# Transposing the gated values of a SwiGLU on VectorE in 32x32 squares instead of on TensorE

## The chip, the cores and the metric

The kernel runs on one core of one Trainium2 chip. The metric is device time in microseconds, the median of several executions; lower is better. One more execution was taken with the hardware profiler. Its rows are what this document reads.

## The reference

Two layers of a decoder trunk over 256 tokens of width 1024, all in float32. Each layer is an attention part (two groups of heads) and then a gated feed-forward part, each between two RMS norms:

```python
D_MODEL = 1024; SEQ = 256; DEPTH = 2
D_FF = -(-8 * D_MODEL // (3 * 256)) * 256          # 2816
...
    x = x + rms_norm(jnp.einsum('bse,ed->bsd', mix, w_out), g_attn_post)
    h = rms_norm(x, g_ffn_pre)
    f = jax.nn.silu(jnp.einsum('bsd,df->bsf', h, w_gate)) * jnp.einsum('bsd,df->bsf', h, w_up)
    x = x + rms_norm(jnp.einsum('bsf,fd->bsd', f, w_down), g_ffn_post)
```

The change lies between the last two lines: f comes out with tokens on partitions, and the product with w_down needs it with its 2816 features on partitions.

## The kernel before, in words

**Products.** Tokens stand in two tiles of 128 (t = 0, 1). Every float32 product is made of three passes of TensorE: an operand is split into a high part and the rest (suffixes h and l), and hh, hl and lh are added up in PSUM (`multiply`, L1083). The weights come in 46 blocks per layer of 1 MB each (128 partitions x 2048 floats), numbered 0 to 45: blocks 13 to 34 are gate and up, 35 to 45 are down. A block is loaded by SP's queue into one of three raw places (L318), ScalarE writes its high part (`hi`, L494) into one of four slots, VectorE subtracts to get the low part (`lo`, L729), and then TensorE may use it, first for tile 0, then for tile 1. `hi` of a block waits until the block four slots back has been used; a load waits until `lo` has read the block three places back. So `after(L, b)` in ScalarE's and VectorE's programs means: the blocks whose slot comes free when TensorE is through with block b. In most of the feed-forward part that is block b + 4. In the down part, where the slots are counted from the end, it is nothing after 34 and 35, block 38 after 36, and blocks 39, 40 and 41 after 37.

**The feed-forward part.** The 2816 features go in six chunks c = 0 to 5: five of 512 features with four blocks each (gate, gate, up, up), and one of 256 features with two. For each chunk and tile ScalarE applies silu to the gate bank (`silus`, L597), VectorE multiplies by up (`swiglu`, L909) and leaves f[t] in SBUF. TensorE then transposes f[t] in 128x128 pieces into PSUM (`f_transposed`, which calls `transpose`, L1123): four pieces per chunk and tile, two in the last chunk. It does this inside the first block of the next chunk, after tile 0 and after tile 1. ScalarE copies the PSUM bank to the high part (`hiT`, L521), VectorE subtracts to get the low part (`loT`, L756). fT (and actT for the last chunk) then is the stationary operand of the down product. The last four down blocks (42 to 45) run for tile 0 first and then for tile 1, and the last two chunks' results are needed only there.

**Order.** Every engine runs its own program, written out by hand, in order; they meet at semaphores. A wait in an engine's program holds up all that stands behind it.

Of the kernel before, what the change touches and what calls it, by code (L numbers as in the profile page):

```python
# [25 lines left out]
P = 128  # L26
D = 1024
T = 2
# [114 lines left out]
for j in range(2):  # L143
    HOLDS[4 + j].append(("ht", 0, j, 1))
    for g in (SWA, MOBA):
        for r in range(3):
# [2 lines left out]
HOLDS[6] += [("ht", 0, 0, 0), ("qk", 0, 0), ("qk", 1, 0), ("qk", 0, 1), ("qk", 1, 1), ("qk", 2, 0), ("qk", 2, 1),  # L149
             ("qk", 3, 0), ("qk", 3, 1), ("mix", SWA, 0), ("mix", SWA, 1), ("mix", MOBA, 0), ("mix", MOBA, 1),  # L150
             ("ht", 1, 0, 0)]
HOLDS[6] += [("ft", c, 0) for c in range(FFN_CHUNKS)]
HOLDS[7] += [("ht", 0, 1, 0), ("pv", SWA, 0), ("pv", SWA, 1), ("pv", MOBA, 0), ("pv", MOBA, 1), ("ht", 1, 1, 0)]
HOLDS[7] += [("ft", c, 1) for c in range(FFN_CHUNKS)]
BANK_OF = {name: b for b in range(8) for name in HOLDS[b]}


def trunk(nc, x_in, b_in, g_attn_pre, g_attn_post, g_moba, g_swa, sinks_in,
# [3 lines left out]
    with ExitStack() as ctx:  # L162
        def sb(name, shape, dt=F32):
            return ctx.enter_context(nc.sbuf_tensor(name, shape, dt))

        def sem(name):
            return ctx.enter_context(nc.semaphore(name))
# [25 lines left out]
        still = work[:, 9, :].bitcast(BF16)  # L193
        silu = [work[:, 6 + t, :] for t in range(T)]
        f = [work[:, 8 + t, :] for t in range(T)]
        v = {MOBA: sb("v_moba", [P, T, GROUP]), SWA: sb("v_swa", [P, T, KV])}
        qT = {g: sb(f"qT_{g}", [P, 4, SEQ]) for g in (MOBA, SWA)}
        kT = {MOBA: sb("kT_0", [P, 4, SEQ]), SWA: sb("kT_1", [P, 1, SEQ])}
# [59 lines left out]
        o_scaled = sem("o_scaled")  # L258
        eps_added = sem("eps_added")
        half_ready = sem("half_ready")  # L260
        pool_step = sem("pool_step")
        dve_step = sem("dve_step")

# [12 lines left out]
        def turned(L, key):  # L276
# [6 lines left out]
        SINK_ARG, SINK_EXP = Order([0, 1]), Order([0, 1])  # L283
        HIT = Order([("ht", 0, 0, 0), ("ht", 0, 0, 1), ("ht", 0, 1, 0), ("ht", 0, 1, 1), ("mix", SWA, 0),
                     ("mix", SWA, 1), ("mix", MOBA, 0), ("mix", MOBA, 1), ("ht", 1, 0, 0), ("ht", 1, 0, 1),
                     ("ht", 1, 1, 0), ("ht", 1, 1, 1)] + [("ft", c, t) for c in range(FFN_CHUNKS) for t in range(T)])

        def transposed(name):

            if name[0] == "ht":  # L290
                return actT, 4 * name[3], 4, name[2]
            if name[0] == "mix":
                return actT, 4 * name[1], 4, name[2]
            if 4 * name[1] < KF_OWN:
                return fT, 4 * name[1], 4, name[2]
            return actT, 4 * name[1] - KF_OWN, KF - 4 * name[1], name[2]

        def tokens(t):
            return slice(t * P, (t + 1) * P)
# [181 lines left out]
        def _(act):  # L481
# [29 lines left out]
            def after(L, b):  # L511

                for c in freed_by(b):
                    hi(L, c)

            def hiT(L, name):

                b = BANK_OF[name]
                dst, k, nk, t = transposed(name)
                act.wait_ge(full[b], HELD[b].done(L, name))  # L520
                nc.scalar.activation(dst["h"][:, k:k + nk, tokens(t)],  # L521
                                     bank[b][:, 0:nk * P].rearrange("p (k n) -> p k n", k=nk), ACT.Copy
                                     ).then_inc(hiT_ready, 1)
                HIT.tick(name)

            def sum_x(L, ph, t):
                into = junk[ph][t] if (L, ph) != (0, 0) else work[:, t, :].bitcast(BF16)
                nc.scalar.activation(into, x[:, t, :], ACT.Square, scale=D ** -0.5,
                                     accum_out=ss_x[:, t:t + 1]).then_inc(squares_x, 1)
                SQ_X.tick((ph, t))  # L530

            def sum_y(L, ph, t, halves=(0, 1)):
                for c in halves:
                    name = ("down" if ph else "out", t, c)
                    b = BANK_OF[name]
                    act.wait_ge(full[b], HELD[b].done(L, name))
                    nc.scalar.activation(y[t][:, c, :], bank[b][:], ACT.Square, scale=D ** -0.5,  # L537
                                         accum_out=ss_y[:, t, c:c + 1]).then_inc(squares_y, 1)
                    SQ_Y.tick((ph, t, c))
# [75 lines left out]
            for L in range(depth):  # L615
# [68 lines left out]
                after(L, 16)  # L684
                for c in range(1, FFN_CHUNKS):
                    b = FIRST_FFN + 4 * c
                    hiT(L, ("ft", c - 1, 0))
                    after(L, b)
                    hiT(L, ("ft", c - 1, 1))
                    silus(L, c, 0)  # L690
                    silus(L, c, 1)
                    for q in range(1, 2 if c == FFN_CHUNKS - 1 else 4):
                        after(L, b + q)
                hiT(L, ("ft", FFN_CHUNKS - 1, 0))
                after(L, FIRST_DOWN)
                hiT(L, ("ft", FFN_CHUNKS - 1, 1))
                for b in range(FIRST_DOWN + 1, NB - 4):
                    after(L, b)
                sum_y(L, 1, 0)
                if L < depth - 1:  # L700
                    hi(L + 1, 0)
# [14 lines left out]
        def _(dve):  # L716
# [15 lines left out]
            def after(L, b):  # L732
                for c in freed_by(b):
                    lo(L, c)
# [16 lines left out]
            def loT(L, name):  # L751

                b = BANK_OF[name]
                dst, k, nk, t = transposed(name)
                dve.wait_ge(hiT_ready, HIT.done(L, name))
                nc.vector.tensor_tensor(dst["l"][:, k:k + nk, tokens(t)],  # L756
                                        bank[b][:, 0:nk * P].rearrange("p (k n) -> p k n", k=nk),
                                        dst["h"][:, k:k + nk, tokens(t)].bitcast(F32), ALU.subtract
                                        ).then_inc(drained[b], 1)
# [140 lines left out]
            def swiglu(L, c, t):  # L900
                n = min(BANK, FF - c * BANK)
                b = BANK_OF["up", c, t]
                dve.wait_ge(full[b], HELD[b].done(L, ("up", c, t)))
                bg = BANK_OF["gate", c, t]
                dve.wait_ge(drained[bg], HELD[bg].done(L, ("gate", c, t)) + 1)
                if c:
                    bt = BANK_OF["ft", c - 1, t]
                    dve.wait_ge(full[bt], HELD[bt].done(L, ("ft", c - 1, t)))
                nc.vector.scalar_tensor_tensor(f[t][:, 0:n], bank[b][:, 0:n], rstd_x[:, t:t + 1], silu[t][:, 0:n],  # L909
                                               ALU.mult, ALU.mult).then_inc(drained[b], 1)  # L910

            nc.vector.memset(still, 0.0).then_inc(still_ready, 1)
            dve.wait_ge(xT_in_done[0], 16)
# [9 lines left out]
            for L in range(depth):  # L923
# [74 lines left out]
                after(L, 14)  # L998
                swiglu(L, 0, 0)
                after(L, 15)  # L1000
                swiglu(L, 0, 1)
                after(L, 16)
                for c in range(1, FFN_CHUNKS):
                    b = FIRST_FFN + 4 * c
                    end = b + (1 if c == FFN_CHUNKS - 1 else 3)
                    loT(L, ("ft", c - 1, 0))
                    after(L, b)
                    loT(L, ("ft", c - 1, 1))
                    for q in range(b + 1, end):
                        after(L, q)  # L1010
                    swiglu(L, c, 0)
                    swiglu(L, c, 1)
                    after(L, end)
                loT(L, ("ft", FFN_CHUNKS - 1, 0))
                after(L, FIRST_DOWN)
                loT(L, ("ft", FFN_CHUNKS - 1, 1))
                for b in range(FIRST_DOWN + 1, NB - 4):
                    after(L, b)
                scale_y(L, 1, 0)
                update_x(L, 1, 0)  # L1020
                if L < depth - 1:
# [18 lines left out]
        def _(pe):  # L1040
# [141 lines left out]
                pe.wait_ge(o_scaled, O_SCALED.done(L, (g, t)))  # L1182
                transpose(L, ("mix", g, t), lambda q: o[t][:, q * P:(q + 1) * P], 4)

            def f_transposed(L, c, t):
                b = BANK_OF["up", c, t]
                pe.wait_ge(drained[b], HELD[b].done(L, ("up", c, t)) + 1)
                transpose(L, ("ft", c, t), lambda q: f[t][:, q * P:(q + 1) * P], min(4, KF - 4 * c))

            def rows_landed(L, ph, t):  # L1190
                for half in range(2):
# [18 lines left out]
            for L in range(depth):  # L1210
# [125 lines left out]
                multiply(L, 1, b + 3)  # L1336
                for c in range(1, FFN_CHUNKS):
                    b = FIRST_FFN + 4 * c
                    multiply(L, 0, b)
                    f_transposed(L, c - 1, 0)  # L1340
                    multiply(L, 1, b)
                    f_transposed(L, c - 1, 1)
                    for q in range(1, 2 if c == FFN_CHUNKS - 1 else 4):
                        multiply(L, 0, b + q)
                        multiply(L, 1, b + q)
                for t in range(T):
                    landed(L, ("ft", FFN_CHUNKS - 2, t))
                for b in range(FIRST_DOWN, NB - 4):
                    multiply(L, 0, b)
                    if b == FIRST_DOWN:  # L1350
                        f_transposed(L, FFN_CHUNKS - 1, 0)
                    multiply(L, 1, b)
                    if b == FIRST_DOWN:
                        f_transposed(L, FFN_CHUNKS - 1, 1)
                for t in range(T):
                    landed(L, ("ft", FFN_CHUNKS - 1, t))
                for b in range(NB - 4, NB):
                    multiply(L, 0, b)
                for b in range(NB - 4, NB):
# [37 lines left out]
```

## Time and profile before

| what | value |
|---|---|
| median of 3 runs | 598.49 us (598.32 to 598.55) |
| the profiled execution: its own time | 598.48 us |
| its span, first to last instruction | 596.7 us |
| TensorE busy | 585.4 us, 98% of the span |
| VectorE busy | 362.0 us, 61% |
| ScalarE busy | 292.8 us, 49% |
| granted TensorE clock | 0.998 of full speed |
| loads | 107.26 MB, mean 180 GB/s |

The profiled execution lies 1.8 us above its span, and 0.01 us from the median, so a microsecond taken from the span is a microsecond taken from the median. Busy shares are averages over stages. Matmuls are pipelined: a recorded duration of one is its passage, not the time that it costs its successor; start to start is what counts there.

### The profile page before, as it was taken

How to read it: one execution, taken by the hardware profiler on the slowest of the kernel's cores; microseconds unless marked ns; L12 is line 12 of the kernel's file. 1: busy time of each engine (PE TensorE's matmuls, PEld its weight loads, DVE VectorE, ACT ScalarE, POOL GpSimd, SP SyncE). 2: the span in 40 equal slices, each digit the busy share in tenths (PEclk: the TensorE clock that was granted, in tenths of full speed). 3: DMA queues.
4: the chain of work that ended last, by engine and by line, in shares of the span. 5: the costliest groups of instructions: out<-in, count | busy, mean ns of one | idle time of the engine just before them, and what ended most of it. 6: DMA issues, size and time to landing. Idle time of an engine off the chain costs nothing.

```text
span 596.7 us, 7657 instructions
## 1 busy us (share of the span) xinstructions
PE 585.4 (98%) x3004; PEld 486.1 (81%) x3004; DVE 362.0 (61%) x469; ACT 292.8 (49%) x417; POOL 42.1 (7%) x68
## 2 busy tenths in 40 slices
PE   7999999999999999999999999999999999999996
PEld 4878887888888889888888888788888888898884
DVE  4888965947536546165497987567645536533632
ACT  6574663755453444153446745665554453424420
POOL 1100001410000000000120100034000000000000
PEclk9999999999999999999999999999999999999999
DMA  8872632437655541559266343507565555342701
GB/s 313 328 239 104 230 142 107 168 125 284 235 168 186 210 154 59 211 224 331 80 239 212 142 159 122 196 6 278 194 244 172 200 171 186 137 184 99 281 1 70
DMA packets 18291, 107.26 MB, mean 180 GB/s; under 512 B 2768, under 2 KB 3024, under 8 KB 6608
## 3 DMA queue, kind: packets, MB, share of 16 engines
q1 hardware_dynamic: 17968, 105.73, 48.9%
q10 hardware_dynamic: 288, 1.05, 0.5%
q8 instruction: 24, 0.39, 0.3%
q14 instruction: 11, 0.09, 0.0%
HBM read 105.72 MB, written 1.05 MB: 179 GB/s over the span
## 4 chain that ended last, share of the span: by engine, by line
PE 85%; DVE 6%; ACT 6%; DMA 1%; issue 1%; DVEq 0%; POOLq 0%; POOL 0%; ACTq 0%
PE bank L1083 75%; PE bank L1123 4%; ACT work L559 3%; DVE w_l L729 3%; PE bank L1173 2%; DVE bank L835 2%; PE bank L1108 2%; ACT w_h L494 2%; PE bank L1148 1%; DMA work<-in_x_first_transposed 1%; DVE actT_l L756 1%; DVE top L835 0%; ACT actT_h L521 0%; ACT work L575 0%; DVE neg_max L839 0%
## 5 line engine op out<-in xcount | busy, mean ns | idle before, releaser
L729 DVE TENSOR_TENSOR w_l<-raw,w_h 128x2048 fp32r<-128x2048 f32 x91 | 207.7, 2290 | 144.2 <-ACT w_h L494 144.1
L494 ACT ACTIVATE w_h<-raw 128x2048 fp32r<-128x2048 f32 x91 | 173.9, 1917 | 143.0 <-PE bank L1083 118.1
L1083 PE MATMUL bank<-w_h,actT_h 128*128 128x512 f32 (+1 forms) x600 | 232.3, 387 | 0.2
L1083 PE MATMUL bank<-w_h,actT_l 128*128 128x512 f32 (+1 forms) x600 | 225.9, 377 | 0.0
L1083 PE MATMUL bank<-w_l,actT_h 128*128 128x512 f32 (+1 forms) x600 | 225.2, 375 | 0.0
L1083 PEld LDWEIGHTS bank<-w_h,actT_h 128*128 128x128 f32 x600 | 113.1, 189 | 22.6 <-issue 2.7
L1083 PEld LDWEIGHTS bank<-w_h,actT_l 128*128 128x128 f32 x600 | 112.9, 188 | 21.2
L1083 PEld LDWEIGHTS bank<-w_l,actT_h 128*128 128x128 f32 x600 | 113.2, 189 | 18.3
L1083 PE MATMUL bank<-w_h,fT_h 128*128 128x512 f32 x160 | 49.8, 392 | 0.0
L1083 PE MATMUL bank<-w_h,fT_l 128*128 128x512 f32 x160 | 49.3, 389 | 0.0
L1083 PE MATMUL bank<-w_l,fT_h 128*128 128x512 f32 x160 | 49.3, 389 | 0.0
L1123 PE MATMUL bank<-ident,work 128*128 128x128 f32 x316 | 46.4, 274 | 2.3 <-ACT work L559 1.5
L1123 PEld LDWEIGHTS bank<-ident,work 128*128 128x128 f32 x316 | 37.4, 141 | 11.5 <-ACT work L559 4.2
L559 ACT ACTIVATE work<-bank,neg_max 128x128 f32<-128x128 f32 (+1 forms) x64 | 26.0, 425 | 33.1 <-DVE neg_max L839 33.1
L1083 PEld LDWEIGHTS bank<-w_l,fT_h 128*128 128x128 f32 x160 | 30.0, 188 | 6.3
L1083 PEld LDWEIGHTS bank<-w_h,fT_l 128*128 128x128 f32 x160 | 30.0, 188 | 6.3
L1083 PEld LDWEIGHTS bank<-w_h,fT_h 128*128 128x128 f32 x160 | 29.5, 188 | 5.8
L444 POOL TENSOR_TENSOR norms<-norms,constants 128x1 f32<-128x1 f32 x8 | 6.8, 844 | 346.6 <-ACT work L537 346.6
L756 DVE TENSOR_TENSOR actT_l<-bank,actT_h 128x512 fp32r<-128x512 f32 (+1 forms) x24 | 14.9, 643 | 23.6 <-ACT actT_h L521 23.6
L597 ACT ACTIVATE work<-bank,norms 128x512 f32<-128x512 f32 (+1 forms) x24 | 15.4, 653 | 22.1 <-PE bank L1083 22.1
L521 ACT ACTIVATE actT_h<-bank 128x512 fp32r<-128x512 f32 (+1 forms) x24 | 12.9, 564 | 27.2 <-PE bank L1123 26.9
L878 DVE TENSOR_TENSOR work<-bank,gain_b 128x512 f32<-128x512 f32 x16 | 10.6, 687 | 24.0 <-ACT work L537 24.0
(73 smaller groups left out, 377.0 us busy)
## 6 DMA issues: line engine op xcount, KB each, us to landing
raw<-in_w_blocks SPq DMA_DIRECT2D x91, 1024.0 KB, 4.9
bias<-in_b_in SPq DMA_DIRECT2D x8, 256.0 KB, 6.3
raw<-in_w_blocks SPq DMA_DIRECT2D x2, 512.0 KB, 7.0
x<-in_x SPq DMA_DIRECT2D x2, 512.0 KB, 14.1
gain_b<-in_g_attn_post SPq DMA_DIRECT2D x2, 512.0 KB, 8.2
bias<-in_g_ffn_pre SPq DMA_DIRECT2D x2, 512.0 KB, 5.6
gain_b<-in_g_ffn_post SPq DMA_DIRECT2D x2, 512.0 KB, 5.6
work<-in_x_first_transposed ACTq DMA_DIRECT2D x1, 516.0 KB, 6.2
```

The lines of the kernel that those rows point to most:

```text
L494: nc.scalar.activation(w["h"][:, slot(b), :], raw[:, r, :], ACT.Copy).then_inc(hi_ready, 1)
L521: nc.scalar.activation(dst["h"][:, k:k + nk, tokens(t)], bank[b][:, 0:nk * P].rearrange("p (k n) -> p k n", k=nk), ACT.Copy).then_inc(hiT_ ...
L559: last = nc.scalar.activation(probs[:, j, n * keys:(n + 1) * keys], bank[4 + j][:, n * keys:(n + 1) * keys], ACT.Exp, bias=neg_max[:, g, t ...
L597: nc.scalar.activation(silu[t][:, 0:n], bank[b][:, 0:n], ACT.Silu, scale=rstd_x[:, t:t + 1]).then_inc(drained[b], 1)
L729: nc.vector.tensor_tensor(w["l"][:, slot(b), :], raw[:, slot(b, RAW), :], w["h"][:, slot(b), :].bitcast(F32), ALU.subtract).then_inc(lo_re ...
L756: nc.vector.tensor_tensor(dst["l"][:, k:k + nk, tokens(t)], bank[b][:, 0:nk * P].rearrange("p (k n) -> p k n", k=nk), dst["h"][:, k:k + nk ...
L835: ins = nc.vector.tensor_tensor_reduce(own, own, mask, SCALE, sinks[:, j, head:head + 1] if g == SWA else NEG, ALU.add, ALU.max, top[:, j, ...
L878: nc.vector.tensor_tensor(y[t][:, c, :], bank[b][:], gain_b[:, c * BANK:(c + 1) * BANK], ALU.mult).then_inc(drained[b], 1)
L1083: ins = nc.tensor.matmul(bank[BANK_OF[name]][:, 0:n], left[s][:, at + k, tokens(t)], right[r][:, k, c * BANK:c * BANK + n], start=first an ...
L1108: ins = nc.tensor.matmul(bank[BANK_OF[name]][:, 0:n], actT[s][:, k, tokens(t)], right[r][:, k, :], start=first, stop=last and (s, r) == pa ...
L1123: ins = nc.tensor.transpose(out_[:, q * P:(q + 1) * P], src(q), ident[:])
L1173: ins = nc.tensor.matmul(bank[b][:, h * HEAD:(h + 1) * HEAD], probsT[:, j, at:at + P], v[g][:, kb, cols], start=kb == 0, stop=kb == blocks ...
```

## The change

The transposes of f leave TensorE. `cross_f` on VectorE turns f[t] by 32x32 squares: for each of the four bands of 32 partitions of the source (i) and each of the four bands of the destination (j) one instruction transposes a row of squares (four of them, or two in the last chunk) into another buffer, `crossed[t]`. That is 16 instructions per chunk and tile, in SBUF. ScalarE's high part (`hi_f`) and VectorE's low part (`lo_f`) then read `crossed[t]` in SBUF, and not a PSUM bank. They come later in their programs: behind the second block of the next chunk, and for the last chunk behind down block 37. TensorE waits for low parts at two places only: for chunk 3 ahead of the down product, for chunk 5 ahead of block 42.

```diff
-HOLDS[6] += [("ft", c, 0) for c in range(FFN_CHUNKS)]
-HOLDS[7] += [("ft", c, 1) for c in range(FFN_CHUNKS)]
+        crossed = [work[:, 4 + t, :] for t in range(T)]
# ScalarE
+            def hi_f(L, c, t):
+                act.wait_ge(crossed_ready[t], f_count(L, c))
+                nc.scalar.activation(f_part("h", c, t), f_view(c, t), ACT.Copy).then_inc(f_hi_ready, 1)
+                F_PARTS.tick((c, t))
...
-                    hiT(L, ("ft", c - 1, 0))
                     after(L, b)
-                    hiT(L, ("ft", c - 1, 1))
                     silus(L, c, 0)
                     silus(L, c, 1)
-                    for q in range(1, 2 if c == FFN_CHUNKS - 1 else 4):
+                    after(L, b + 1)
+                    hi_f(L, c - 1, 0)
+                    hi_f(L, c - 1, 1)
+                    for q in range(2, 2 if c == FFN_CHUNKS - 1 else 4):
                         after(L, b + q)
...
# VectorE
                 if c:
-                    bt = BANK_OF["ft", c - 1, t]
-                    dve.wait_ge(full[bt], HELD[bt].done(L, ("ft", c - 1, t)))
+                    dve.wait_ge(crossed_ready[t], f_count(L, c - 1))
...
+            def cross_f(L, c, t):
+                b = BANK_OF["up", c, t]
+                n = P * f_blocks(c)
+                dve.wait_ge(drained[b], HELD[b].done(L, ("up", c, t)) + 1)
+                if L or c:
+                    dve.wait_ge(f_lo_ready, F_PARTS.before(L, (c, t)) - 1)
+                into = crossed[t][:, 0:n].rearrange("p (k n) -> p k n", n=P)
+                for i in range(4):
+                    for j in range(4):
+                        ins = nc.vector.transpose(into[32 * j:32 * j + 32, :, 32 * i:32 * i + 32],
+                                                  f[t][32 * i:32 * i + 32, 0:n].rearrange("p (k j b) -> p j k b", j=4,
+                                                                                          b=32)[:, j])
+                ins.then_inc(crossed_ready[t], 1)
+            def lo_f(L, c, t):
+                dve.wait_ge(f_hi_ready, F_PARTS.done(L, (c, t)))
+                nc.vector.tensor_tensor(f_part("l", c, t), f_view(c, t), f_part("h", c, t).bitcast(F32), ALU.subtract
+                                        ).then_inc(f_lo_ready, 1)
...
                 swiglu(L, 0, 0)
                 after(L, 15)
+                cross_f(L, 0, 0)
                 swiglu(L, 0, 1)
                 after(L, 16)
+                cross_f(L, 0, 1)
                 for c in range(1, FFN_CHUNKS):
                     b = FIRST_FFN + 4 * c
                     end = b + (1 if c == FFN_CHUNKS - 1 else 3)
-                    loT(L, ("ft", c - 1, 0))
                     after(L, b)
-                    loT(L, ("ft", c - 1, 1))
                     for q in range(b + 1, end):
                         after(L, q)
+                        if q == b + 1:
+                            lo_f(L, c - 1, 0)
+                            lo_f(L, c - 1, 1)
+                    if c == FFN_CHUNKS - 1:
+                        lo_f(L, c - 1, 0)
+                        lo_f(L, c - 1, 1)
                     swiglu(L, c, 0)
                     swiglu(L, c, 1)
+                    cross_f(L, c, 0)
                     after(L, end)
-                loT(L, ("ft", FFN_CHUNKS - 1, 0))
-                after(L, FIRST_DOWN)
-                loT(L, ("ft", FFN_CHUNKS - 1, 1))
-                for b in range(FIRST_DOWN + 1, NB - 4):
+                    cross_f(L, c, 1)
+                for b in range(FIRST_DOWN, NB - 4):
                     after(L, b)
+                    if b == FIRST_DOWN + 2:
+                        lo_f(L, FFN_CHUNKS - 1, 0)
+                        lo_f(L, FFN_CHUNKS - 1, 1)
# TensorE
-            def f_transposed(L, c, t):
-                b = BANK_OF["up", c, t]
-                pe.wait_ge(drained[b], HELD[b].done(L, ("up", c, t)) + 1)
-                transpose(L, ("ft", c, t), lambda q: f[t][:, q * P:(q + 1) * P], min(4, KF - 4 * c))
+            def f_landed(L, c):
+                pe.wait_ge(f_lo_ready, F_PARTS.done(L, (c, T - 1)))
...
-                    multiply(L, 0, b)
-                    f_transposed(L, c - 1, 0)
-                    multiply(L, 1, b)
-                    f_transposed(L, c - 1, 1)
-                    for q in range(1, 2 if c == FFN_CHUNKS - 1 else 4):
+                    for q in range(2 if c == FFN_CHUNKS - 1 else 4):
                         multiply(L, 0, b + q)
                         multiply(L, 1, b + q)
-                for t in range(T):
-                    landed(L, ("ft", FFN_CHUNKS - 2, t))
+                f_landed(L, FFN_CHUNKS - 3)
...
+                f_landed(L, FFN_CHUNKS - 1)
```

## Rows read from the trace of the kernel before

**Rows 1.** The page: busy time, and TensorE's share of the chain that ended last

```profile
PE 585.4 (98%) x3004; PEld 486.1 (81%) x3004; DVE 362.0 (61%) x469; ACT 292.8 (49%) x417; POOL 42.1 (7%) x68
PE 85%; DVE 6%; ACT 6%; DMA 1%; issue 1%; DVEq 0%; POOLq 0%; POOL 0%; ACTq 0%
```

**Rows 2.** Chain in order of time, chunk 2 of layer 0: start, length, what

```profile
142.64 0.44 PE bank L1123 x4
143.08 19.08 PE bank L1083 x84
162.16 0.44 PE bank L1123 x4
162.59 2.77 PE bank L1083 x12
165.37 0.44 PE bank L1123 x4
```

**Rows 3.** VectorE's timeline over one chunk: start, length, instruction, [idle before, releaser]

```profile
182.19 0.75 DVE L909 SCALAR_TENSOR_TENSOR work<-bank,norms,work 128x512 f32<-128x512 f32 x1 [0.48 <-PE bank L1083]
184.21 2.29 DVE L729 TENSOR_TENSOR w_l<-raw,w_h 128x2048 fp32r<-128x2048 f32 x1 [1.26 <-ACT w_h L494]
186.41 0.68 DVE L756 TENSOR_TENSOR fT_l<-bank,fT_h 128x512 fp32r<-128x512 f32 x1
190.14 2.29 DVE L729 TENSOR_TENSOR w_l<-raw,w_h 128x2048 fp32r<-128x2048 f32 x1 [3.04 <-ACT w_h L494]
192.34 0.68 DVE L756 TENSOR_TENSOR fT_l<-bank,fT_h 128x512 fp32r<-128x512 f32 x1
```

**Rows 4.** VectorE's timeline near the start: operations of 128 and 64 elements

```profile
21.46 0.29 DVE L810 TENSOR_TENSOR work<-work,sin 128x128 f32<-128x128 f32 x1
21.67 0.28 DVE L811 TENSOR_TENSOR work<-work,cos 128x128 f32<-128x128 f32 x1
21.99 0.23 DVE L814 TENSOR_TENSOR work<-work 128x64 f32<-128x64 f32 x1
22.13 0.22 DVE L816 TENSOR_TENSOR work<-work 128x64 f32<-128x64 f32 x1
```

**Rows 5.** VectorE's timeline where chunk 0 of layer 0 ends

```profile
136.46 2.28 DVE L729 TENSOR_TENSOR w_l<-raw,w_h 128x2048 fp32r<-128x2048 f32 x1
138.66 0.75 DVE L909 SCALAR_TENSOR_TENSOR work<-bank,norms,work 128x512 f32<-128x512 f32 x1
```

**Rows 6.** Chain in order of time, from TensorE's first transposes of f

```profile
125.82 13.60 PE bank L1083 x60
139.43 0.44 PE bank L1123 x4
```

**Rows 7.** Chain in order of time, chunk 5 and the down product of layer 0

```profile
230.48 0.44 PE bank L1123 x4
230.92 2.88 PE bank L1083 x24
233.80 0.44 PE bank L1123 x4
234.23 8.51 PE bank L1083 x60
242.74 0.22 PE bank L1123 x2
242.96 2.75 PE bank L1083 x12
245.71 0.22 PE bank L1123 x2
245.93 48.99 PE bank L1083 x216
```

**Rows 8.** ScalarE's timeline: the high part of block 38

```profile
251.50 1.92 ACT L494 ACTIVATE w_h<-raw 128x2048 fp32r<-128x2048 f32 x1 [5.15 <-PE bank L1083]
```

**Rows 9.** SP's queue: who it waited for (us in total, times, longest)

```profile
SPq L312 <- DVE w_l L729: 497.6, 84, 18.1
```

**Rows 10.** DMA issues, KB each, median us from issue to landing

```profile
raw<-in_w_blocks SPq DMA_DIRECT2D x91, 1024.0 KB, 4.9
```

More of the change, by code:

```diff
@@ L260, in trunk @@
         half_ready = sem("half_ready")
+        crossed_ready = [sem(f"crossed_ready{t}") for t in range(T)]
+        f_hi_ready = sem("f_hi_ready")
+        f_lo_ready = sem("f_lo_ready")
         pool_step = sem("pool_step")
@@ L285, in trunk @@
                      ("mix", SWA, 1), ("mix", MOBA, 0), ("mix", MOBA, 1), ("ht", 1, 0, 0), ("ht", 1, 0, 1),
-                     ("ht", 1, 1, 0), ("ht", 1, 1, 1)] + [("ft", c, t) for c in range(FFN_CHUNKS) for t in range(T)])
+                     ("ht", 1, 1, 0), ("ht", 1, 1, 1)])
+        F_PARTS = Order([(c, t) for c in range(FFN_CHUNKS) for t in range(T)])
         def transposed(name):
@@ L296, in transposed, with f_blocks, f_count, f_view @@
             return actT, 4 * name[1] - KF_OWN, KF - 4 * name[1], name[2]
+        def f_blocks(c):
+            return min(4, KF - 4 * c)
+        def f_count(L, c):
+            return L * FFN_CHUNKS + c + 1
+        def f_view(c, t):
+            return crossed[t][:, 0:f_blocks(c) * P].rearrange("p (k n) -> p k n", n=P)
+        def f_part(s, c, t):
+            dst, k, nk, _ = transposed(("ft", c, t))
+            return dst[s][:, k:k + nk, tokens(t)]
         def tokens(t):
@@ L686, in _ @@
                     b = FIRST_FFN + 4 * c
-                    hiT(L, ("ft", c - 1, 0))
                     after(L, b)
-                    hiT(L, ("ft", c - 1, 1))
                     silus(L, c, 0)
                     silus(L, c, 1)
-                    for q in range(1, 2 if c == FFN_CHUNKS - 1 else 4):
+                    after(L, b + 1)
+                    hi_f(L, c - 1, 0)
+                    hi_f(L, c - 1, 1)
+                    for q in range(2, 2 if c == FFN_CHUNKS - 1 else 4):
                         after(L, b + q)
-                hiT(L, ("ft", FFN_CHUNKS - 1, 0))
-                after(L, FIRST_DOWN)
-                hiT(L, ("ft", FFN_CHUNKS - 1, 1))
-                for b in range(FIRST_DOWN + 1, NB - 4):
+                for b in range(FIRST_DOWN, NB - 4):
                     after(L, b)
+                    if b == FIRST_DOWN + 2:
+                        hi_f(L, FFN_CHUNKS - 1, 0)
+                        hi_f(L, FFN_CHUNKS - 1, 1)
                 sum_y(L, 1, 0)
@@ L1005, in _ @@
                     end = b + (1 if c == FFN_CHUNKS - 1 else 3)
-                    loT(L, ("ft", c - 1, 0))
                     after(L, b)
-                    loT(L, ("ft", c - 1, 1))
                     for q in range(b + 1, end):
                         after(L, q)
+                        if q == b + 1:
[4 more added lines that the diff above has]
+                        lo_f(L, c - 1, 1)
                     swiglu(L, c, 0)
                     swiglu(L, c, 1)
+                    cross_f(L, c, 0)
                     after(L, end)
-                loT(L, ("ft", FFN_CHUNKS - 1, 0))
-                after(L, FIRST_DOWN)
-                loT(L, ("ft", FFN_CHUNKS - 1, 1))
-                for b in range(FIRST_DOWN + 1, NB - 4):
+                    cross_f(L, c, 1)
+                for b in range(FIRST_DOWN, NB - 4):
                     after(L, b)
+                    if b == FIRST_DOWN + 2:
+                        lo_f(L, FFN_CHUNKS - 1, 0)
+                        lo_f(L, FFN_CHUNKS - 1, 1)
                 scale_y(L, 1, 0)
@@ L1338, in _ @@
                     b = FIRST_FFN + 4 * c
-                    multiply(L, 0, b)
-                    f_transposed(L, c - 1, 0)
-                    multiply(L, 1, b)
-                    f_transposed(L, c - 1, 1)
-                    for q in range(1, 2 if c == FFN_CHUNKS - 1 else 4):
+                    for q in range(2 if c == FFN_CHUNKS - 1 else 4):
                         multiply(L, 0, b + q)
                         multiply(L, 1, b + q)
-                for t in range(T):
-                    landed(L, ("ft", FFN_CHUNKS - 2, t))
+                f_landed(L, FFN_CHUNKS - 3)
                 for b in range(FIRST_DOWN, NB - 4):
                     multiply(L, 0, b)
-                    if b == FIRST_DOWN:
-                        f_transposed(L, FFN_CHUNKS - 1, 0)
                     multiply(L, 1, b)
[L1353 to L1356, printed above, removed]
+                f_landed(L, FFN_CHUNKS - 1)
                 for b in range(NB - 4, NB):
```

## The prediction

> **What bounds the kernel now.** I read the page first: TensorE is busy for 98% of the span and carries 85% of the chain that ended last [rows 1]. Then the chain in order of time: in the feed-forward part it is TensorE and nothing else, matmuls and small groups of transposes without a gap [rows 2]. So this stage is bound by TensorE, and what leaves TensorE comes off the time, as long as the engines that feed it keep up. Last VectorE's timeline over one chunk: its four `lo` each start when ScalarE's high part is there, with 1 to 3.5 us idle before them [rows 3]. That idle time is the cover under which the new work must fit.
>
> **What TensorE gains.** From one group of transposes to the same group a chunk later the chain takes 165.37 - 142.64 = 22.73 us; in it stand 96 matmuls and two groups [rows 2]. The 84 matmuls without a break take 19.08 us, 0.227 us each, so 96 take 21.80 us, and a group costs 0.465 us (0.44 in its row, the rest in the matmul behind it). There are 2 layers x 5 chunks x 2 tiles = 20 such groups, and 4 small ones of the last chunk at 0.22 to 0.25 us [rows 7]. Gain: 20 x 0.465 + 4 x 0.245 = 10.3 us, all of it on the path. With it alone the time is 598.5 - 10.3 = 588.2 us.
>
> **What one step costs VectorE.** The trace has no 32x32 transpose, so I bound a step by the nearest rows. A full step has 128 elements per partition (4 squares), a step of the last chunk 64. An operation of 128 elements takes 0.28 to 0.29 us, and its successor, if it waits for nothing, starts 0.21 us after it (21.46 to 21.67); if it waits for its predecessor's result, 0.32 us after it (21.67 to 21.99) [rows 4]. For 64 elements it is 0.14 and about 0.255 us (0.225 and the same 0.03). Lower end: steps overlap like ordinary ones, t = 0.21. Upper end: turning a square makes an engine take in 32 elements before the first comes out; 64 elements more cost 0.065 us by these rows, 32 more 0.033, so t = 0.353. I take 0.32 and 0.255. The pair that overlaps reads and writes the same 128 partitions; each of the 16 steps writes to another band than the one before, which no row shows, and I take for it the row in which one operation starts when the other is through.
>
> The Trainium skill has a rule on exactly this (VectorE: DVE Perf Modes, "Two Vector instructions with no wait between them"): an instruction whose output starts in another quadrant of partitions than the last one's starts only when all earlier ones have finished. No row here shows such an instruction. The same page ("The three transpose paths") gives 311 ns for a 128x128 bf16 transpose on VectorE; as an estimate from that figure, in the sum below, there would be no stall and 588.2 us.
>
> **Does VectorE keep up?** Start to start, VectorE needs per full chunk 4 x 2.20 for `lo` (184.21 to 186.41), 2 x 0.67 for `swiglu` and 2 x 0.61 for the low parts of f (their 0.75 and 0.68 less the overlap of 0.08) [rows 3]: 11.4 us. With 32 steps of 0.32 it is 21.6 us against TensorE's 21.8. It just fits, with 99% of VectorE taken; above t = 0.325 VectorE loses ground in every chunk. `hi_f` and `lo_f` replace copies of the same size, ScalarE is half idle, and they are needed only in the down product; I cost them at nothing beyond this.
>
> What is late next? Let T be the time at which TensorE starts a chunk. VectorE's queue then holds: `swiglu` of tile 1, 16 steps, one `lo`, 16 steps, and then `lo` of the block that opens the next chunk. That one starts at T + 0.04 + 0.67 + 2.20 + 32t = T + 2.9 + 32t = 13.1, is through at 15.4, and TensorE wants it at 21.8: 6.4 us in hand. SP's queue waits for `lo` nearly always [rows 9], so the load behind this `lo` moves too: it lands 4.9 us later [rows 10], at 20.3, and ScalarE wants it at 21.8, while VectorE comes to that block only 5.8 us after that. So a lateness of up to some 5 us in the chunks costs TensorE nothing.
>
> The lateness starts in chunk 0. There `cross_f` of tile 0 stands ahead of `swiglu` of tile 1 and behind a `lo`: it starts at 138.66 [rows 5]. TensorE starts chunk 1 at 139.43 - 2.73 = 136.70 (12 matmuls ahead of the group) [rows 6]. The 32 steps end at 1.96 + 0.67 + 2.20 + 32t = 4.84 + 32t, 1.9 us behind the steady state; by the like rows of layer 1, 1.6. I take 1.8. Each of the four chunks that follow adds 32t - 10.4 = -0.16: 1.8 - 0.64 = 1.1 us of lateness are left when chunk 5 begins.
>
> **Where it bites.** Chunk 5 has only two blocks, and its 32 steps come upon those of chunk 4. From TensorE's start of block 33 VectorE has: 2.9 + 32t, `lo` of 37 (2.20), two `lo_f` (1.22), two `swiglu` of 256 columns (0.8), 32 steps of 0.255, and then `lo` of block 38 (2.29), and 0.05 for the signal: 9.5 + 10.2 + 8.2 + 1.1 of lateness = 29.0 us. TensorE wants block 38 after two blocks of 5.77 (8.51 for 60 matmuls, less 12 of 0.227) and three of 5.44: 27.9 us [rows 7]. Before, the high part of 38 began when block 36 was used, at 251.50 [rows 8], and the pair took 4.2 of 5.4 us; now VectorE comes to it 1.2 us too late. In general the stall per layer is 192t - 60.3 with the small step 0.065 below the full one (128t from four chunks, 64t from the last stretch), nothing below t = 0.314. At 0.32 it is 1.1 to 1.2 us. Behind it the work is `lo` alone, each with its slack, so it isn't paid twice. The last low parts wait behind block 41, some 8 us ahead of block 42.
>
> **Sum.** -10.3 + 2 x 1.15 = -8.0 us, on the profiled execution 590.5 us; its own time, 598.48, is the median's, so the median too: 590.5 us.
>
> **The rivals.**
> - *The steps overlap* (t of 0.21, or up to 0.314): no stall, 588.2 us. For it: every ordinary pair in the trace without a wait overlaps. Against: the changing bands. Chance 0.30.
> - *The steps are slower and VectorE becomes the bound* (the other side): it decides from t = 0.341, where two stalls of 5.15 us eat the gain; every 0.01 us on a step is 3.8 us. At the upper end, 0.353, it is 2 x 7.5 - 10.3 = +4.7, 603 us. For it: VectorE would stand at 99% already, and the filling of the squares is priced nowhere. Against: it needs both that addition and no overlap. Chance 0.18.
> - *A step takes each 4-byte element twice*: 256 elements, 0.42 us by the like of the slope above (64 to 128 elements: 0.065), 0.45 with the wait, 0.32 for the small ones: 1.8 + 4 x 4.1 + 32 x 0.77 - 18.4 = 24.5 us of stall per layer, +39, 637 us. Nothing in the rows speaks for it. Chance 0.07.
> - *The gain isn't there*, TensorE's groups having hidden something, or the stall about equals it (t of 0.338 to 0.344): 598.5 us. The chain has no gap at the groups, so the first is unlikely. Chance 0.08.
> - My forecast, t between 0.314 and 0.337: 588.2 to 597 us. Chance 0.37.
>
> **How the numbers follow.** What this kernel's measurement can tell from no change is about 0.2%, 1.2 us. Faster by more: 0.30 + 0.37 = 0.67, less a little for what I haven't seen: 0.66. Same 0.08. Slower 0.18 + 0.07, and that little: 0.26. The range begins just below the full gain, 587.8, and goes to 602: it leaves out the doubled step and the worse half of the slower steps, less than 2 in 10. The likeliest case's own range is 588.2 to 597.
>
> **What would show it.** TensorE should have no L1123 left in the feed-forward part and 21.8 us per chunk. The new transposes on VectorE should start every 0.32 us, and every 0.255 in chunk 5; VectorE should be almost without idle time from chunk 0 to block 38. The chain should leave TensorE once per layer, for `lo` of block 38. If VectorE has idle time in each chunk, the steps overlap; if the chain leaves TensorE in chunks 2 to 4, or the load of a block follows a late `lo` into it, they are slower than I think, and the prediction falls on the high side.

## The result, and the profile after

The changed kernel takes 605.95 us (median of 4 runs, 604.82 to 606.23), before 598.5 us: 1.0121 times as long, interval 1.0104 to 1.0139. It is slower by 7.5 us where 8.0 us less was forecast.

The page of the changed kernel's profile, against [rows 1]: span, busy time, and the chain that ended last.

```profile
span 602.7 us, 7863 instructions
PE 578.9 (96%) x2916; PEld 480.1 (80%) x2916; DVE 469.0 (78%) x853; ACT 292.8 (49%) x417; POOL 42.4 (7%) x68
PE 49%; DVE 38%; ACT 6%; issue 5%; DMA 1%; DVEq 0%; POOLq 0%; POOL 0%; ACTq 0%
```

TensorE has less to do (88 instructions fewer), and yet the span is 6.0 us longer. VectorE carries 38% of the chain in place of 6%. Who TensorE waited for (us in total, times, longest), the first two rows:

```profile
PE bank L1138 <- DVE work L935: 12.6, 2, 6.4
PE bank L1178 <- ACT work L585: 1.5, 4, 0.8
```

The first row is new: two waits, one per layer, 12.6 us together; L935 is `swiglu` (L909 before). The second one, in the attention part, is the same in the kernel before. VectorE is now busy for 469.0 us in place of 362.0. VectorE's timeline of the changed kernel where the first one falls, to be held against [rows 3]:

```profile
202.34 1.41 DVE L935 SCALAR_TENSOR_TENSOR work<-bank,norms,work 128x512 f32<-128x512 f32 x2
203.66 5.04 DVE L948 STREAM_TRANSPOSE work<-work 32x128 f32<-32x128 f32 x16
208.73 2.29 DVE L756 TENSOR_TENSOR w_l<-raw,w_h 128x2048 fp32r<-128x2048 f32 x1
...
223.82 1.41 DVE L935 SCALAR_TENSOR_TENSOR work<-bank,norms,work 128x512 f32<-128x512 f32 x2
225.14 5.03 DVE L948 STREAM_TRANSPOSE work<-work 32x128 f32<-32x128 f32 x16
230.21 2.29 DVE L756 TENSOR_TENSOR w_l<-raw,w_h 128x2048 fp32r<-128x2048 f32 x1
232.42 5.05 DVE L948 STREAM_TRANSPOSE work<-work 32x128 f32<-32x128 f32 x16
237.50 2.29 DVE L756 TENSOR_TENSOR w_l<-raw,w_h 128x2048 fp32r<-128x2048 f32 x1
239.71 1.28 DVE L956 TENSOR_TENSOR fT_l<-work,fT_h 128x512 fp32r<-128x512 f32 x2
240.91 0.87 DVE L935 SCALAR_TENSOR_TENSOR work<-bank,norms,work 128x256 f32<-128x256 f32 x2
241.69 7.98 DVE L948 STREAM_TRANSPOSE work<-work 32x64 f32<-32x64 f32 x32
```

No idle time stands in it. A full step costs (5.04 - 0.30) / 15 = 0.316 us start to start, a small one (7.98 - 0.24) / 31 = 0.25; a chunk (202.34 to 223.82) takes VectorE 21.5 us. The products of chunk 5 come at 240.91. And TensorE's timeline at the same time:

```profile
234.83 0.28 PE L1138 MATMUL bank<-w_h,actT_l 128*128 128x256 f32 x1
241.53 1.19 PE L1138 MATMUL bank<-w_h,fT_h 128*128 128x512 f32 x2 [6.42 <-DVE work L935]
242.52 1.06 PE L1138 MATMUL bank<-w_l,fT_h 128*128 128x512 f32 x2
243.38 1.06 PE L1138 MATMUL bank<-w_h,fT_l 128*128 128x512 f32 x2
...
246.10 0.63 PE L1138 MATMUL bank<-w_h,fT_h 128*128 128x512 f32 x2
246.57 0.62 PE L1138 MATMUL bank<-w_l,fT_h 128*128 128x512 f32 x2
```

TensorE ends block 34 at 235 and starts the down product at 241.53, right behind the first product of chunk 5 (240.91 + 0.49). Then there is a second loss: pairs of matmuls start 0.86 us apart at first, and 0.46 from 246 on. The table by stretches has the length, then busy time and number of instructions of TensorE, its weight loads, VectorE, ScalarE and GpSimd, then the granted TensorE clock as a share of full speed, and last the busy share of the DMA engines and what they moved in GB/s:

```profile
235.20:241.50 6.30, 0.00 (x0) 0.00 (x0) 6.17 (x13) 0.63 (x1) 0.00 (x0) 0.76 0.01 5
241.53:246.10 4.57, 4.57 (x12) 3.67 (x13) 4.32 (x19) 0.00 (x0) 0.00 (x0) 0.59 0.99 409
246.10:250.00 3.90, 3.90 (x19) 3.21 (x18) 3.38 (x15) 0.00 (x0) 0.00 (x0) 1.00 0.77 319
```

Where does TensorE's gain go, then? The removed groups give 10.3 us, the two waits take 12.6, and the slow matmuls behind each take 4.57 - 12 x 0.227 = 1.85 us in the first layer (56.45 us for the 240 matmuls to the next group, where 240 x 0.227 would be 54.5, so up to 2 us) and about as much in the second (61.90 for 264). With 2 us each that is 12.6 + 4.0 - 10.3 = +6.3 us, and the profiled execution is at 604.82, 6.3 above the one before.

### The profile page after: what moved, and what is told of

Its sections match the earlier page's. It is cut to its first block, busy times and chain, and to the rows that moved or that the text cites. A ratio compares the mean times of both kernels' runs of the same rounds, so it can differ in the third digit from the quotient of the medians.

```text
span 602.7 us, 7863 instructions
## 1 busy us (share of the span) xinstructions
PE 578.9 (96%) x2916; PEld 480.1 (80%) x2916; DVE 469.0 (78%) x853; ACT 292.8 (49%) x417; POOL 42.4 (7%) x68
## 4 chain that ended last, share of the span: by engine, by line
PE 49%; DVE 38%; ACT 6%; issue 5%; DMA 1%; DVEq 0%; POOLq 0%; POOL 0%; ACTq 0%
PE bank L1138 40%; DVE work L948 15%; DVE w_l L756 15%; ACT work L585 3%; PE bank L1178 3%; DVE work L935 2%; PE bank L1228 2%; ACT w_h L514 2%; DVE bank L862 2%; PE bank L1163 2%; DVE fT_l L956 2%; PE bank L1203 1%; DMA work<-in_x_first_transposed 1%; DVE actT_l L783 1%; DVE top L862 0%
## 5 line engine op out<-in xcount | busy, mean ns | idle before, releaser
L948 DVE STREAM_TRANSPOSE work<-work 32x128 f32<-32x128 f32 (+1 forms) x384 | 111.8, 291 | 5.0
L1138 PE MATMUL bank<-w_h,fT_h 128*128 128x512 f32 x160 | 51.4, 403 | 12.6 <-DVE work L935 12.6
L1138 PEld LDWEIGHTS bank<-w_h,fT_h 128*128 128x128 f32 x160 | 30.8, 194 | 19.2 <-DVE fT_l L956 12.9
L1178 PE MATMUL bank<-ident,work 128*128 128x128 f32 x228 | 33.0, 275 | 2.3 <-ACT work L585 1.5
L1178 PEld LDWEIGHTS bank<-ident,work 128*128 128x128 f32 x228 | 26.5, 141 | 8.9 <-ACT work L585 4.3
L783 DVE TENSOR_TENSOR actT_l<-bank,actT_h 128x512 fp32r<-128x512 f32 x20 | 13.2, 687 | 12.7 <-ACT actT_h L541 12.7
```

The lines of the kernel that those rows point to most:

```text
L783: nc.vector.tensor_tensor(dst["l"][:, k:k + nk, tokens(t)], bank[b][:, 0:nk * P].rearrange("p (k n) -> p k n", k=nk), dst["h"][:, k:k + nk ...
L948: ins = nc.vector.transpose(into[32 * j:32 * j + 32, :, 32 * i:32 * i + 32], f[t][32 * i:32 * i + 32, 0:n].rearrange("p (k j b) -> p j k b ...
L1138: ins = nc.tensor.matmul(bank[BANK_OF[name]][:, 0:n], left[s][:, at + k, tokens(t)], right[r][:, k, c * BANK:c * BANK + n], start=first an ...
L1178: ins = nc.tensor.transpose(out_[:, q * P:(q + 1) * P], src(q), ident[:])
```

## The experiments

**1. The down product's sums in other PSUM banks.** `multiply` claims a bank before its first matmul, and a claim waits until the last user of that bank is through. The down product of tile 0 adds up in banks 2 and 3, and bank 3 holds up of chunk 5 until `swiglu` has read it. Banks 6 and 7 are free in the feed-forward part since the change, and so is bank 5, which takes one of tile 1's sums in place of bank 1, the up bank of tile 1.

```diff
-for c in range(2):
-    HOLDS[2 + c].append(("down", 0, c))
-    HOLDS[c].append(("down", 1, c))
...
+DOWN_BANKS = ((6, 7), (0, 5))
+for t in range(T):
+    for c in range(2):
+        HOLDS[DOWN_BANKS[t][c]].append(("down", t, c))
```

> Edit: the changed kernel with the down product's sums in other PSUM banks: tile 0 in banks 6 and 7, tile 1 in banks 0 and 5, in place of 2, 3 and 0, 1. Nothing on VectorE changes. Theory A (the wait is for a bank: TensorE may not start the down product before VectorE has read the last up bank of chunk 5, which it reaches 5.8 us late): both idle times of 6.4 us go, and the slow matmuls behind them; what is left is the stall at block 38 that was forecast, 0.5 to 1.2 us per layer. 589.4 us, between 588 and 591. Rival B (VectorE is full, so its lateness is paid wherever it is looked for; the wait only moves): the time stays above 600 us and the same idle time shows up at a later block. Rival C (TensorE waits for the low parts of f, not for a bank): no change, 606 us.

589.92 us (589.77 to 590.01), 0.9855 times before (0.9841 to 0.987). This one edit on PSUM, with VectorE's program untouched, is worth 16 us. Who TensorE waited for, of this kernel:

```profile
PE bank L1139 <- DVE w_l L757: 1.0, 2, 0.6
```

Two waits of half a microsecond, for `lo`: the stall at block 38 that the prediction had in its sum. VectorE's row for it, and the chain from there on:

```profile
249.93 2.29 DVE L757 TENSOR_TENSOR w_l<-raw,w_h 128x2048 fp32r<-128x2048 f32 x1
```

```profile
249.93 2.30 DVE w_l L757
252.28 38.43 PE bank L1139 x168
```

Theory A stands; B and C fall: VectorE is as full as in the changed kernel (busy 469.2 against 469.0 us), and the time is 0.5 us above the 589.4 expected.

**2. And block 38 ahead of the last 16 steps.**

```diff
                     cross_f(L, c, 0)
                     after(L, end)
+                    if c == FFN_CHUNKS - 1:
+                        after(L, FIRST_DOWN)
+                        after(L, FIRST_DOWN + 1)
                     cross_f(L, c, 1)
                 for b in range(FIRST_DOWN, NB - 4):
-                    after(L, b)
+                    if b > FIRST_DOWN + 1:
+                        after(L, b)
```

> Edit: as the kernel with the other banks, and on VectorE the low part of weight block 38 is put ahead of the last 16 steps of chunk 5. Theory A: no wait of TensorE is left in the feed-forward part; the full gain of the removed transposes, 588.3 us, 1 to 2 us below the kernel with the other banks alone. Rival B (VectorE full): no difference between the two.

588.31 us (588.18 to 588.4), 0.9829 times before (0.9814 to 0.9843). The chain of this kernel in order of time:

```profile
221.94 67.81 PE bank L1143 x344
289.74 0.87 PE bank L1183 x8
```

From the end of chunk 4 to the next layer's transposes it is TensorE without a break. The gain is the 10.3 us that the removed groups were priced at (598.5 - 588.3 = 10.2), and 1.6 us of it came from this edit (589.92 to 588.31).

**3. The products of chunk 5 sooner, in the old banks.**

```diff
-                    after(L, b)
+                    if c == FFN_CHUNKS - 1:
+                        swiglu(L, c, 0)
+                        swiglu(L, c, 1)
+                    else:
+                        after(L, b)
...
+                    if c < FFN_CHUNKS - 1:
+                        swiglu(L, c, 0)
+                        swiglu(L, c, 1)
                     if c == FFN_CHUNKS - 1:
+                        after(L, b)
                         lo_f(L, c - 1, 0)
                         lo_f(L, c - 1, 1)
-                    swiglu(L, c, 0)
-                    swiglu(L, c, 1)
```

> Edit: the changed kernel, old banks; on VectorE the two products of chunk 5 stand ahead of the low part of block 37 and of the low parts of f of chunk 4. Theory A: VectorE reaches the product of tile 0 some 3.4 to 3.6 us sooner, so each idle time falls from 6.4 to about 3 us: 606.0 - 2 x 3.5 = 599 us if the matmuls behind the wait stay slow for 2 us, 595 us if the shorter idle time no longer lowers the granted clock. Rival C (low parts of f): these come later or no sooner, 606 us or more.

597.59 us (median of 10 runs, 596.13 to 598.82), between the two times expected of theory A; C falls. TensorE's waits:

```profile
PE bank L1144 <- DVE work L935: 5.8, 2, 3.0
```

The idle time falls by 6.8 us. The median falls by 8.4, the profiled executions by 6.9 (604.82 to 597.93), so the idle time accounts for the difference of the profiled ones by itself. The 599 us were for slow matmuls behind the wait, the 595 for none, and the stretches show them still there:

```profile
238.43:242.38 3.95, 3.95 (x11) 3.10 (x12) 3.94 (x6) 0.00 (x0) 0.00 (x0) 0.57 0.25 33
242.38:246.00 3.62, 3.62 (x17) 3.00 (x16) 3.40 (x15) 0.00 (x0) 0.00 (x0) 1.00 0.90 376
```

An idle time of 3.0 us brings a granted clock of 0.57 for 3.95 us, in which 10 matmuls start that take 2.3 us at the full clock: 1.7 us lost, nearly as much as behind 6.4 us. The loads stood at 33 GB/s just then.

**4. Matmuls in the wait.** The changed kernel with work for TensorE ahead of the down product; it adds nothing to the result.

```diff
                 f_landed(L, FFN_CHUNKS - 3)
+                for _ in range(26):
+                    nc.tensor.matmul(bank[6][:], actT["h"][:, 7, tokens(1)], w["h"][:, slot(FIRST_DOWN - 1), 0:BANK],
+                                     start=True, stop=True)
```

> Edit: the changed kernel, with 26 matmuls of 512 columns into the unused bank 6 ahead of the down product, 5.9 us at 0.227 us each, so that TensorE works for most of the wait. They add nothing to the result. Theory: of the loss, the part behind the wait is the granted clock (0.58 in the 4.5 us after it, matmuls every 0.43 us in place of 0.227): with TensorE kept at work the clock stays at 1.0 and 2 x 2.0 us come back, 602 us, while the wait for VectorE itself stays. Rival: the matmuls behind the wait are slow for another reason, such as the loads that run at 408 GB/s at that moment: 606 us, and the slow spacing is still there.

601.66 us (601.3 to 601.89), 4.3 us under the changed kernel by the medians. The profiled executions are 2.9 us apart (604.82 and 601.89); about 0.5 us of what is missing was lost before this place (TensorE starts the last matmul of block 34 at 235.33 here and at 234.83 there). The stretches:

```profile
235.20:241.50 6.30, 6.30 (x30) 4.94 (x28) 6.16 (x13) 0.63 (x1) 0.00 (x0) 1.00 0.04 8
241.50:246.00 4.50, 3.96 (x18) 3.29 (x18) 4.29 (x19) 0.00 (x0) 0.00 (x0) 1.00 0.88 366
```

18 matmuls in place of 12 in those 4.5 us, with the clock at 1.00 and the loads at 366 GB/s. So it was the idleness of TensorE and not the loads that slowed them. The time spent waiting for VectorE stays lost (the added matmuls fill it); only what the clock cost behind it is given back.

**5. Steps that stay in one band.** The output is another one: the squares are turned, but don't reach the other bands.

```diff
-                for i in range(4):
-                    for j in range(4):
+                for j in range(4):
+                    for i in range(4):
                         ins = nc.vector.transpose(into[32 * j:32 * j + 32, :, 32 * i:32 * i + 32],
-                                                  f[t][32 * i:32 * i + 32, 0:n].rearrange("p (k j b) -> p j k b", j=4,
-                                                                                          b=32)[:, j])
+                                                  f[t][32 * j:32 * j + 32, 0:n].rearrange("p (k i b) -> p i k b", i=4,
+                                                                                          b=32)[:, i])
```

> Edit: the changed kernel; each step transposes squares within one band of 32 partitions (source band = destination band), band by band, so that in 3 of 4 steps neither the band read nor the band written changes. The squares do not reach the bands where they belong, so the output is another one; the number and size of the steps are the same. Theory H (it is the change of band that keeps a step from starting before the one ahead is through): start to start falls from 0.316 us to 0.21 to 0.24 us where the band stays, 0.24 us in the mean; VectorE then has 2.4 us more per chunk, the product of chunk 5 comes sooner and the wait of 6.4 us falls to about 3 us: 597 to 599 us. Rival N (transposes never overlap, whatever their bands): 0.316 us and 606 us.

597.17 us (595.63 to 597.52). VectorE's timeline:

```profile
180.34 0.75 DVE L935 SCALAR_TENSOR_TENSOR work<-bank,norms,work 128x512 f32<-128x512 f32 x1 [0.48 <-PE bank L1138]
181.01 3.58 DVE L948 STREAM_TRANSPOSE work<-work 32x128 f32<-32x128 f32 x16
```

16 steps in 3.58 us in place of 5.04, (3.58 - 0.27) / 15 = 0.22 us start to start, and VectorE waits for TensorE in the chunks again. The wait of TensorE is 5.3 us in the two layers, and the time as expected. The steps one by one tell more than the mean. The fourth and the fifth, between which the band changes:

```profile
181.62 0.26 DVE L948 STREAM_TRANSPOSE work<-work 32x128 f32<-32x128 f32 x1
181.90 0.30 DVE L948 STREAM_TRANSPOSE work<-work 32x128 f32<-32x128 f32 x1
```

The fifth starts 0.28 us after the fourth, 0.02 behind its end; the ninth and the thirteenth do the same, within 0.01. The 12 others start 0.19 to 0.24 us after the one ahead, before it has ended.

**6 and 7. Only one side changes its band.** 6 reads the first band always (`f[t][0:32, 0:n]` for `f[t][32 * i:32 * i + 32, 0:n]`), so it leaves out three quarters of f. 7 exchanges the loops, `for j` outside and `for i` inside, and computes the same as the changed kernel.

> Edit: the changed kernel; each step reads the first band, and writes to another band each time. Three quarters of f are left out, the steps are as many and as long. Theory H: 0.316 us start to start, since the band written changes at every step. If it is the band read alone that holds a step: 0.21 to 0.24 us. Rival N: 0.316 us.

> Edit: the changed kernel with the two loops over bands exchanged: the same 16 steps in another order, in which the band read changes at every step and the band written at every fourth. Theory H: 0.316 us, since a change on either side holds a step. If it is the band written alone: 0.24 us in the mean, and 597 to 599 us. Rival N: 0.316 us.

605.89 and 604.1 us, one run each. The 16 steps of 6 and of 7 on VectorE's timelines:

```profile
181.91 5.03 DVE L948 STREAM_TRANSPOSE work<-work 32x128 f32<-32x128 f32 x16
```

```profile
181.94 5.04 DVE L948 STREAM_TRANSPOSE work<-work 32x128 f32<-32x128 f32 x16
```

0.315 and 0.316 us. Either change, of the band read or of the band written, is enough, and an order of the 16 steps that spares only one side gains nothing. One more rival is that a step from one band into another is slow by itself, whatever stood ahead of it. The rows speak against it: no step of experiment 5 leaves its band, and still those at a change start only when the one ahead is through; and in the changed kernel the steps that stay in their band (i = j) follow each other and their neighbours at the same 0.30 to 0.32 us as the rest.

**8. 20 steps in place of 16**, on the fast version of experiment 2.

```diff
                 into = crossed[t][:, 0:n].rearrange("p (k n) -> p k n", n=P)
+                for j in range(4):
+                    source = 32 * ((j + 1) % 4)
+                    nc.vector.transpose(rope_tmp[32 * j:32 * j + 32, 0:n].rearrange("p (k n) -> p k n", n=P)[:, :, 32 * t:32 * t + 32],
+                                        f[t][source:source + 32, 0:n].rearrange("p (k n) -> p k n", n=P)[:, :, 0:32])
```

> Edit: the fast version (other banks, block 38 ahead) with 4 more steps ahead of the 16, into unused scratch, 20 per chunk and tile. It tests how thin VectorE's margin is. By the sum: 11.4 + 40 x 0.316 = 24.0 us of VectorE per chunk against TensorE's 21.8, so it loses 2.2 us in each of four chunks; with 1.8 us from chunk 0 and 0.8 us in hand at block 38 the stall is 10 us per layer: 588.3 + 20 = 608 us, plus up to 2 us per layer if the granted clock falls at the waits. The waits should be for low parts of weight blocks, and not for a bank. Rival (VectorE still has room, the 1.5% margin is not real): within 2 us of 588.3 us.

615.57 us (614.83 to 616.04), 27.3 above the version without them. TensorE's waits for low parts, and those of its weight loads (PEld):

```profile
PE bank L1147 <- DVE w_l L757: 18.0, 11, 3.6
```

```profile
PEld bank L1147 <- DVE w_l L757: 23.0, 12, 4.0
```

Now the waits are for the weight blocks, in the chunks themselves, as expected of a VectorE that is the bound. The size was set too low: 20 to 24 expected. A chunk takes VectorE 24.3 us (two of them from 186.74 to 235.27) and not 24.0. The waits themselves are near the 20 us expected: 18.0 us for `lo` and 0.7 for a product. But TensorE is busy for 583.0 us with the same 2916 matmuls that take 574.6 in experiment 2. These 8.4 us, the 18.7 and 0.5 more at waits of the attention part are the 27.6 us between the two spans (613.8 and 586.2). A good part of the 8.4 is the clock (0.991 in the mean against 0.997): after a wait of 2.21 us that ends at 205.53, matmuls start 0.43 us apart in place of 0.227, from 206.80 to 209.79. How much the rest of the waits add in this way isn't separated here.

## Why the prediction was wrong

**What TensorE gains: right.** 10.3 us forecast, 10.2 measured in experiment 2, where nothing takes it back.

**What a step costs: right.** 0.32 and 0.255 us forecast, 0.316 and 0.25 measured. Of the two rows the slower one was the right one to take, against the pair that overlaps [rows 4]: experiments 5 to 7 give 0.22 us where both bands mostly stay, 0.316 where either changes. The rule on quadrants of the Trainium skill ("VectorE: DVE Perf Modes", "Two Vector instructions with no wait between them") names both sides, the start of an input and that of the output, and these runs agree with it. The upper end that I had for a step, an extra 0.033 us for filling a square, was mostly absent: a step of 128 elements lasts 0.302 us, 0.01 to 0.02 more than an ordinary operation of 128 elements.

**What VectorE does and when: right.** 21.6 us per chunk forecast, 21.5 measured. From the forecast's own terms the first product of chunk 5 comes 2.9 + 10.2 + 2.2 + 1.2 + 1.1 = 17.6 us behind the start of block 33. TensorE is through with block 34 at 235, two blocks of 5.77 us behind that start, so the start is at 223.5, and 240.91 is 17.4 behind it.

**The stall at block 38: there, but smaller.** Forecast 1.15 us per layer; in experiment 1 the waits are 0.6 us at most, and taking the stall away in experiment 2 gives 1.6 us for the two layers, 0.8 each. In the changed kernel it can't be seen, since the earlier wait pushed TensorE behind it.

**The step that failed is "Where it bites".** It followed what TensorE waits for among the weight blocks and the low parts of f, and left out the PSUM banks. The first down block claims the banks of gate and up of tile 0, and the up bank is free only when `swiglu` of chunk 5 has read it. I had that `swiglu` in the list, at 17.6 us, and TensorE at the down product at 11.5; the difference, 6.1 us, is the wait (12.6 us in the two layers, 6.4 the longer one) and stood in no sum: a term put at nothing without a reason. Experiment 1 shows it: with the sums in other banks both waits are gone, and 16 us with them. Before, the same claim cost nothing. Tile 0's product of chunk 5 on VectorE and the first matmuls of the down product on TensorE, in the kernel before:

```profile
238.65 0.47 DVE L909 SCALAR_TENSOR_TENSOR work<-bank,norms,work 128x256 f32<-128x256 f32 x1
239.83 0.63 PE L1083 MATMUL bank<-w_h,fT_h 128*128 128x512 f32 x2
```

The product was through at 239.12, 0.7 us before TensorE wanted its bank. VectorE's new work moved it some 7 us back against TensorE's place, these 0.7 and the 6.4 of the wait. I had costed that lateness for the weight blocks and the low parts alone.

**And a second term, the clock.** An idle time of 6.4 us cost more than itself: the matmuls behind it ran with a granted clock of 0.59 for 4.6 us (pairs 0.86 us apart in place of 0.46; that is the lower of the two levels, 1.2 GHz in place of 2.4, for most of the stretch), 1.85 to 2 us per layer. Experiment 4 shows that it was TensorE's idleness: with matmuls in the wait, 4.3 us come back by the medians, 2.9 by the profiled executions. The prediction had no such term either.

**The rival on the other side had the right sign for another reason.** It wanted slower steps, from 0.341 us on, and even at its upper end it came to 603 us. The steps were not slower. The range ended at 602 because the only way to a slower kernel in it was a step that costs more; a wait that I hadn't listed had no place in it.

**Open:** the profiled execution, 604.82 us, is the lowest of its four; the others are 1 to 1.4 us above it, at the same granted clock. Nothing here says where that lies.

## What to carry to other kernels

Work that is put on an engine with room makes everything behind it late, so list each semaphore that this engine raises, each bank it sets free among them, with the new time beside the time at which somebody wants it; a busy share that still fits says nothing about that. Where a lateness is found at a bank, another bank may be cheaper than another order: with the down sums in banks that the change itself had freed, the same 16 steps give 588.3 us, 1.7% under the kernel before. And price an idle time of TensorE with the clock behind it.

## What was not expected of the hardware

- After 6.4 us without a matmul TensorE's granted clock was 0.59 for 4.6 us, and after 3.0 us it was 0.57 for 3.95 us: more than halving the wait gave back little of that cost. With 26 matmuls in the same place the clock stayed at 1.00. In experiment 8 a wait of 2.21 us was enough, and the slow matmuls came only 1.3 us after TensorE had started again.
- A change of the band of 32 partitions on either side, read or written, makes the next VectorE transpose start 0.316 us after the last, 0.01 us behind its end; in experiment 5, where the one ahead is shorter, 0.28 us after it; without a change it starts 0.19 to 0.24 us after it. The recorded duration goes with it: 0.30 us for a step at a change, 0.26 for one without (experiment 5).
